# Queries and keys of a gated delta rule kept by features, with their norms and decays as broadcast rows instead of transposes in every chunk

## The reference

```
lower = where(strict, (k*beta) @ k^T * decay, 0);  tinv = (lower + I)^-1
u = tinv @ (v*beta);   w = tinv @ (k*beta*exp(g))
qk = where(causal, q @ k^T * decay, 0)
v_new = u - w @ state
o = (q*exp(g)) @ state + qk @ v_new
state = state * exp(g_last) + (k*exp(g_last - g))^T @ v_new
```

## Time and profile before

| | us |
|---|---|
| median of 3 runs | 1813.22 (1810.52 to 1816.22) |
| the profiled execution, device time | 1814.77 |
| its span from first to last instruction | 1812.9 |
| PE busy | 1732.7 (96%) |
| DVE, ACT, POOL busy | 910.4, 662.6, 483.4 |

### The profile page before, as it was taken

How to read it: one execution, slowest core, us unless ns; L and a number is a source line. 1 busy time by engine, 2 the same in 40 slices (tenths; PEclk the granted TensorE clock), 3 DMA queues, 4 the chain that set the end, 5 groups by cost and what they waited for, 6 DMA issues and landing times.

```text
span 1812.9 us, 31814 instructions
## 1 busy us (share of the span) xinstructions
PE 1732.7 (96%) x12561; PEld 1661.0 (92%) x12561; DVE 910.4 (50%) x1007; ACT 662.6 (37%) x1081; POOL 483.4 (27%) x470
## 2 busy tenths in 40 slices
PE   6999999986999999999969989999999999999997
PEld 6999999976999999999969989999999999999996
DVE  5454444563455544554452355455455455455457
ACT  6444474344455445444432342122222212212213
POOL 3222222223444354334402112122122122222220
PEclk9999999998999999999989999999999999999998
DMA  6233333224233423344295102111111111111112
GB/s 184 74 87 92 91 87 95 78 96 149 68 90 97 124 85 96 72 120 118 69 283 169 32 17 61 44 43 61 35 47 57 35 55 49 35 58 46 35 46 93
DMA packets 209164, 148.38 MB, mean 82 GB/s; under 512 B 43165, under 2 KB 197556, under 8 KB 207973
## 3 DMA queue, kind: packets, MB, share of 16 engines
q1 hardware_dynamic: 168052, 116.24, 22.3%
q10 hardware_dynamic: 40848, 31.49, 5.7%
q0 software_dynamic: 224, 0.12, 0.0%
HBM read 110.25 MB, written 37.58 MB: 82 GB/s over the span
## 4 chain that ended last, share of the span: by engine, by line
PE 80%; DVE 6%; issue 4%; DVEq 3%; DMA 2%; ACT 2%; POOL 1%; POOLq 1%; SPq 0%; ACTq 0%
PE gb L717 60%; PE db L1044 8%; PE db L853 3%; DVEq L1459 3%; PE db L850 2%; PE db L770 1%; DVE h L1841 1%; DMA yo<-ot_d 1%; PE db L923 1%; PE db L922 1%; DVE cacc L1496 1%; DVE hx L1769 1%; POOL w_lo L614 1%; PE db L997 1%; DVE fino L1875 0%
## 5 line engine op out<-in xcount | busy, mean ns | idle before, releaser
L717 PE MATMUL gb<-u_hi,w_hi 128*128 128x342 f32 (+2 forms) x2520 | 827.1, 328 | 17.1 <-ACT ht L1368 6.6
L717 PE MATMUL gb<-u_lo,w_hi 128*128 128x342 f32 (+2 forms) x2520 | 811.8, 322 | 0.0
L717 PE MATMUL gb<-u_hi,w_lo 128*128 128x342 f32 (+2 forms) x2520 | 808.5, 321 | 0.0
L614 POOL TENSOR_TENSOR w_lo<-w_raw,w_hi 128x1024 fp32r<-128x1024 f32 x128 | 327.1, 2564 | 1043.6 <-ACT w_hi L1086 1043.6
L717 PEld LDWEIGHTS gb<-u_hi,w_hi 128*128 128x128 f32 x2520 | 479.2, 190 | 21.5 <-issue 18.7
L717 PEld LDWEIGHTS gb<-u_lo,w_hi 128*128 128x128 f32 x2520 | 479.7, 190 | 0.4
L717 PEld LDWEIGHTS gb<-u_hi,w_lo 128*128 128x128 f32 x2520 | 479.0, 190 | 0.0
L1841 DVE TENSOR_TENSOR h<-h,db 128x512 f32<-128x512 f32 x176 | 117.5, 685 | 56.9 <-PE db L1044 56.5
L1044 PE MATMUL db<-w_hi,a_hi 128*128 128x512 f32 x352 | 139.6, 397 | 4.3 <-DVE a_lo L1865 2.9
L1086 ACT ACTIVATE w_hi<-w_raw 128x1024 fp32r<-128x1024 f32 x128 | 133.5, 1052 | 14.7 <-ACT tm L1176 13.0
L1044 PE MATMUL db<-w_hi,a_lo 128*128 128x512 f32 x352 | 138.2, 393 | 0.0
(11 more groups left out here) (236 smaller groups left out, 1855.3 us busy)
## 6 DMA issues: line engine op xcount, KB each, us to landing
w_raw<-in_w_in SPq DMA_DIRECT2D x53, 512.0 KB, 4.3
w_raw<-in_w_up SPq DMA_DIRECT2D x44, 512.0 KB, 3.8
qkv_d<-tm ACTq DMA_DIRECT2D x24, 576.0 KB, 3.4
tk<-qkv_d SPq DMA_DIRECT2D x9, 1536.0 KB, 7.2
w_raw<-in_w_down SPq DMA_DIRECT2D x22, 512.0 KB, 3.3
ot_d<-ots ACTq DMA_DIRECT2D x9, 512.0 KB, 3.2
yb_d<-ybs ACTq DMA_DIRECT2D x8, 513.0 KB, 3.9
yl<-yb_d SPq DMA_DIRECT2D x8, 513.0 KB, 5.5
```

The lines of the kernel that those rows point to most:

```text
L614: pool.tensor_tensor(w_lo[:, n % SLOTS, :], w_raw[:, n % SLOTS, :], w_hi[:, n % SLOTS, :].bitcast(F32), ALU.subtract).then_inc(s_wlo, 1)
L717: mm = pe.matmul(gb[:, bank, 0:w], wt, u, start=(k == 0 and m == 0), stop=(k == KT - 1 and m == 2))
```

## The change

Queries and keys are stored a second time by features: ACT stores `sl` to `qkT_d` before it is transposed, and only keys and values go by tokens to `kv_d`. The norm and beta of a key (`FKB`) and g (`GCUM`) are turned to rows once, by two PE transposes in the pooling stage (`rowsb`, stored to `rows_d`). For each chunk SP loads `kT` and `qT` from `qkT_d` and the two rows broadcast to all 128 partitions (`brow`, `grow`). DVE multiplies them: `kbt` = `kT` x `brow`, `ex` = `grow` - mask, `kgt` = `kbt` x exp(`grow`), `qdt` = `qT` x exp(`grow`). The key's own norm in `ex` comes as a logarithm added to g (`GLN`); the query's norm is applied to the output (`FQ`, `FQ2`). The six transpose steps and their copies are gone.

KK of the next chunk is now the first step of an iteration, and the 27 pieces lie differently behind the steps. `bds` goes back, and the loads for the chunk after follow, after the load of `tk`. In the pooling stage KK of chunk 0 stands before the fourth projection, so the blocks of the first inverse are solved during the pooling products. The last iteration is written out apart from the loop; on DVE the first too.

```diff
-STEPS = ["P1", "TKN", "V", "TKB", "GROW", "KK", "TQ", "TKG", "O", "SU", "QK", "TQD", "OT"]
+STEPS = ["KK", "P1", "V", "O", "SU", "QK", "OT"]
...
-FILLS = {"P1": 2, "TKN": 0, "V": 1, "TKB": 0, "GROW": 1, "KK": 2, "TQ": 2, "TKG": 2, "O": 2, "SU": 2, "QK": 1,
-         "TQD": 2, "OT": 3, "X0": 1, "Y0": 2, "X1": 1, "Y1": 1, "X2": 1, "Y2": 1}
+FILLS = {"KK": 2, "P1": 2, "V": 2, "O": 3, "SU": 2, "QK": 2, "OT": 3, "X0": 2, "Y0": 2, "X1": 2, "Y1": 2, "X2": 1,
+         "Y2": 2}
...
+FIRST_PLAN = [("pool", j) for j in range(5)] + ["QK"] + [("pool", j) for j in range(5, KT)]
...
+            sp.wait_ge(s_plo, 4)
+            load_tk(0)
+            sp.wait_ge(s_ps["QK"], 2)
+            load_kT(1)
+            load_qT(1)
+            blocks_back(0)
...
+            def chunk_loads(n, last):
+                blocks_out(n)
+                sp.wait_ge(s_vb, n)
+                sp.wait_ge(s_kd, n)
+                load_tk(n)
+                blocks_back(n)
+                if not last:
+                    sp.wait_ge(s_ps["QK"], 2 * n + 2)
+                    load_kT(n + 1)
+                    sp.wait_ge(s_kb, n + 1)
+                    sp.wait_ge(s_qd, n + 1)
+                    load_row(brow, 1, n + 1, s_br)
+                    load_row(grow, 0, n + 1, s_gr)
+                    load_qT(n + 1)
...
+            def key_rows(c):
+                dve.wait_ge(s_kT, 16 * c + 16)
+                dve.wait_ge(s_br, 16 * c + 16)
+                dve.tensor_tensor(kbt[:, :, :], kT[:, :, :], brow[:, :, :], ALU.mult).then_inc(s_kb, 1)
...
+                    if name == "P1" and isinstance(i, int) and i == 0:
+                        first_inverse()
+                    if not last and name == "Y0":
+                        key_rows(i + 2)
+                    elif not last and name == "X1":
+                        decays(i + 2)
```

More of the change, by code:

```diff
@@ L681, in _, with chunk @@
             state_parts(0)
[L682 to L686, removed]
+            w_low(W_ZG + 1)
+            pool.wait_ge(s_sst, 32)
+            w_low(W_ZG + 2)
+            def chunk(i, last):
                 substitute(i + 1)
+                if not last:
+                    pool.wait_ge(s_ev["QK"], 2 * i + 4)
+                    mask(i + 2)
                 pool.wait_ge(s_ps["SU"], 2 * i + 2)
@@ L915, in step @@
                     pe.wait_ge(s_ev["SU"], 2 * c + 2)
-                    each([done["TKG"]], product(kgt, st))
+                    pe.wait_ge(s_kg, c + 1)
+                    each([], product(kgt, st))
                 elif name == "V":
@@ L923, in both @@
                         return pe.matmul(o, qkm[:, m, :], vv[:, m, :], start=False, stop=True)
-                    each([done["V"], done["QK"], done["TQD"]], both)
+                    pe.wait_ge(s_qd, c + 1)
+                    each([done["V"], done["QK"]], both)
                 elif name == "SU":
@@ L975, in _ @@
                         piece(p, i)
+            with pe.Fori(0, HEADS - 1) as i:
+                chunk(i)
+            chunk(HEADS - 1)
             for name, prev in (("P1", LAST_Y), ("V", "P1"), ("O", "V"), ("OT", "O")):
@@ L1267, in copy_halves, with act_step @@
                     act.activation(heads(dst, h), dbank(name, h), ACT.Copy).then_inc(s_ev[name], 1)
-            def act_step(name, c):
-                if name == "TQ":
-                    copy_halves(name, qnt, c)
-                elif name == "TKN":
-                    copy_halves(name, knt, c)
-                elif name == "TQD":
-                    copy_halves(name, qdt, c)
-                elif name == "TKG":
-                    copy_halves(name, kgt, c)
-                elif name == "GROW":
-                    for h in range(2):
-                        act.wait_ge(s_ev[name], 2 * c + h + 1)
-                        act.activation(heads(ex, h), heads(ex, h), ACT.Exp).then_inc(s_dec, 1)
+            def act_step(name, c, last=False):
+                if name == "Y1" and not last:
+                    decays(c + 1)
                 elif name == "Y0":
@@ L1340, in _ @@
                 act.wait_ge(s_za, 16 * i + 16)
+            with act.Fori(0, HEADS - 1) as i:
+                chunk(i, False)
+            chunk(HEADS - 1, True)
             for name in REC:
@@ new lines, in _, with first_inverse @@
+            dve_step("QK", 0)
+            drain()
+            dve.tensor_tensor(ex[:, :, :], per_head(factor(GLN, 1)), over_heads(cst[:, C_NEG:C_NEG + P]),
+                              ALU.add).then_inc(s_nm, 1)
+            key_rows(1)
+            drain()
+            decays(1)
+            dve.drain().then_inc(s_ev[LAST_Y], 2)
+            def first_inverse():
+                dve.wait_ge(s_bd, 16)
+                dve.wait_ge(s_zero, 5)
+                for p in range(P // SQ):
+                    t = dve.transpose(rr[square(p), :, square(p)], bds[square(p), :, :])
+                t.then_inc(s_rd, 1)
```

440 lines of the change are left out of this document (244 added, 196 removed).

## The result

The changed kernel takes 1821.45 us (median of 7 runs, 1815.34 to 1823.92) against 1813.22: ratio 1.004, 95% interval 1.0023 to 1.0056. It is slower, by about 8 us (0.4%). The profiled execution is its fastest run, 1815.34 us with a span of 1813.5.

A forecast was written before the change was run, and what follows sets the result against it. PE alone was taken to bound the loop at 58.85 us an iteration. A 17.0 us gain at the start plus 7 x (58.85 - 55.2) = 25.6 gave 42.6, so 1772.2 profiled, 1771 median; range 1752 to 1794.

The forecast's parts named there:

- PE's own work: Chunk loop: 48 transposes removed save PE 5.7 us an iteration, so its period falls from 58.85 to 53.15 us.
- The chain from `gs` to POOL: Loop: weights issue to T + 7.4, blocks land T + 14.4 behind them, POOL starts T + 17.1.
- The substitution: POOL's solve in the loop: 12.9 us, plus 1.0 us for steps held by DVE products of two SBUF tiles.
- the strict reading: POOL's substitution: each DVE product with two SBUF inputs counts its full 1.25 us or so, giving a period of 56.6.
- Solution out and back: ... 5.1 us: Loop, from the substitution's end to X0: solution stored, reloaded and transposed in 5.1 us, so X0 can start at T + 35.1.
- The period is then 35.1 + 19.05: Loop: X0 at T + 35.1 plus 19.05 us of PE work behind it, 54.15 us; with POOL's held steps 55.2.
- the rival of the longer chain: Loop: weights and blocks crowd, period 57 to 60, time 1783 to 1804; chance 0.20 for 1782 to 1808.
- I leave its end at 418.7: Pooling stage: ACT's eight scalings start 1 us later but end as before; last store lands 422.6, P1 of chunk 0 at 425.0.
- The bound for this, 5 us: Pooling stage: QK and the loads of `kT` and `qT` may stretch the scalings by 5 us, cutting the gain to 12.
- The gain of 17.0: Start to end of iteration 0: ends at 479.5 in place of 496.47, 17.0 us gained, bounds 12 and 21.
- The broadcast rows: Loop: rival that row loads come late and PE stops before X1 and Y1 copies; 1837 us at 20 us landing; chance 0.06.
- The change moves nothing: Loop: rival that the way of the blocks eats just the transposes' time, needing a period near 61 us; chance 0.02.

The follow-up runs named there:

- the first experiment: On the changed kernel, SP sends the inverse's blocks out and back ahead of the three weight loads in the chunk loop: 1789.32 us, ratio 0.9872.
- that edit's base: Changed kernel with blocks ahead of weights, pooling-stage loads moved, and one gate-projection piece moved from behind OT to between QK and OT: 1770.67 us, ratio 0.9761.
- loads moved: On the changed kernel, chunk 0's QK right behind KK, so kT and qT load before the pooling stores; tk loads behind the last scaling: 1812.75 us, ratio 1.0008.
- the fastest version: Blocks first, pooling-stage loads moved, one piece moved ahead of OT; then chunk 0's KK and QK put behind the fourth pooling projection: 1763.54 us, ratio 0.9719.

## Why the prediction was wrong

1. **PE's own work: right.** 48 transposes for 5.7 us and a period of 53.15 without waits; 53.12 was measured once nothing else held the loop. By the mean duration of 275 ns it would have been 45.7.

2. **The chain from `gs` to POOL: right.** Forecast and measured, from KK at T: weights issued T + 7.4 and T + 8.0; blocks landed T + 14.4 and about T + 14.1, where their loads start; POOL's start T + 17.1 and T + 17.4. The first experiment shows what this queue order costs together with points 4 and 5, 4.3 us an iteration; without these two, with the outputs stored late, the order leaves 55.3 us, as forecast.

3. **The substitution: nearly right.** 12.9 + 1.0 = 13.9 forecast, 14.3 measured (631.59 to 645.87), with three held steps of 0.75, 1.02 and 1.17. A product costs up to 0.9 us, not the 1.25 of the strict reading of the Trainium skill (GPSIMD Engine Reference, Specifications); that fewer were allowed for is 0.4 us. The other direction, POOL's product holding one of DVE's, wasn't priced; by the traces it is behind the wait at OT in the first experiment, and behind the 3.1 and 3.4 us of `kbt` and `ex` of chunk 0 at the start.

4. **"Solution out and back: ... 5.1 us": the first failing step.** It was taken from the iteration before the change, where the way was clear. The change moved the solution later, onto ACT's 512 KB store of the outputs, and the two small stores then took 3.5 us in place of 1.7 and 1.9. From 645.90 to the end of `rrs` at 652.66 it was 6.8 us. X0 started at T + 38.6, PE was there at T + 34.25 (forecast 34.1). The prediction priced no meeting of DMAs from two engines on this leg. The Trainium skill (DMA: Bandwidth & Descriptors, Issuing engines are not separate DMA queues) says that DMAs of all issuing engines run on the same engines and interleave; the landing times here, 3.5 us beside the large store and 1.7 with it late, agree with that.

5. **"The period is then 35.1 + 19.05": the second failing step.** The 19.05 us behind X0 were matmuls at full clock. After a stop of 4.3 us part of them ran at 1.2 GHz, and X0 to KK took 21.2 us; where no stop of that length came before (X0 at 595.53) it took 18.7. With points 3 and 4 that is 59.74 for this iteration and 58.5 in the mean, against 55.2 forecast: 7 x 3.3 = 23 us. Summed over the seven, X0 starts 15.6 us too late, and what follows it takes 7.9 us too long. It ended in the rival of the longer chain (57 to 60), but for a cause that the rival didn't name; weights and blocks didn't crowd.

6. **"I leave its end at 418.7": the largest failing step.** The last store of the scalings was to land at 422.6 and landed at 439.0, 16.4 us later. By the rows: 5.6 us because the first started later, 8.7 because they stretched, 2.1 for the last one's landing (6.0 in place of 3.9). In all twelve changed versions P1 of chunk 0 starts 2.7 us behind this last landing (forecast 2.4), so the stores decide. The prediction let the scalings start 1 us later and end as before. They start late by PE's wait for `kbt` and the slow clock behind it, with KK ahead of the fourth projection, and, once that is gone, by DVE's products for chunk 0 ahead of the last pooled sums. With KK and QK behind the fourth projection the first store comes at 402.4, 1.5 us earlier than in the changed kernel (3.0 earlier than in that edit's base, where QK stood ahead too); the other 4.1 us are DVE's by the trace, and no run moved them. The stretch is the loads of `tk`, `kT` and `qT`: undone, 20.3 us remain of 29.1. The bound for this, 5 us, was worked from QK and the loads of `kT` and `qT`, and `tk` was overlooked. P1 of chunk 0 came at 441.8 in place of 425.0, iteration 0 ended at 500.7 in place of 479.5: 21 us, of which 4.4 lie behind P1. There the forecast had X0 wait for the third weight slot and the blocks, until 460.4; X0 started at 482.01 without a wait, and PE waited 4.3 us for `rr` in its place, which the prediction hadn't. The gain of 17.0 became a loss of 4.2.

The sum: 23 + 21 - 1.5 (the tail behind the last P1 was that much shorter) = 43 us, and the profiled run was to be 1772.2 and was 1815.3. That the median lies 6.1 us above the profiled run, where it lay 1.6 below, is the other 7.7 of the miss.

7. **The rivals and the signs.** The broadcast rows aren't late: `brow` and `grow` land 6.2 and 7.4 us after issue, like weights, and PE never waits at X1 to X2. "The change moves nothing" needed a period near 61; the time came out near that with 58.5, because the start lost what it was to win. Two signs of the forecast's own chain came: PE's repeated wait is the one before X0, ended by `rrs`, and the blocks land right behind the third weights. Of the signs of error, one came: the pooling stage ended behind 425, though by loads beside its stores and a late start, not by `bds`; with `bds` at 419 to 421 (loads moved) P1 still came at 435 to 438. The wait at OT on DVE's scaling isn't among the loop's repeated waits in the changed kernel; it comes when the blocks go first.

Left open: of the 6.8 us by which P1 of chunk 0 is still behind the forecast in the fastest version, 6.5 are the stores (402.4 to a last landing at 429.1). Why they land in 4.9 us in the median, and not in 4.3, with few loads beside them wasn't tried; nor was moving DVE's products for chunk 0 in the fastest version, or POOL's product away from DVE's small one.

## What to carry to other kernels

When an edit takes work from the bounding engine and hangs a chain through DRAM on the same loop, list every DMA of every engine by time and ask which ones the moved chain will now meet; here a small store issued 0.4 us behind a large one landed only when the large one had (3.5 us in place of 1.7). Price a new wait on PE twice, once for the wait and once for the matmuls behind it. When an edit makes one of POOL and DVE start its work earlier or later, look at what the other then does in the same microsecond. Where the start of a kernel is a pipeline of stores, put no load beside it and nothing that waits for another engine ahead of the matmuls that feed it.

## What the hardware showed unexpectedly

- **A large store doubles the landing time of small ones beside it.** Two stores of 32 KB land in 1.7 and 1.9 us alone and in 3.5 when 512 KB were issued 0.4 us before (the large one landed 3.8 us after its issue, just ahead of them); issued 0.8 and 0.5 us ahead of the large one they land in 1.7 and 1.9. Being ahead by less isn't enough: in the iteration with the stores at 764.05 and 764.40 and the large one at 764.46 the first lands in 1.7 us and the second in 3.8.
- **Stores beside loads.** The first `yb_d` store, 513 KB, took 9.1 us beside the 1 MB load of `tk`, and 4.5 without it.
- **The clock behind a wait.** The 15 matmuls behind X0 took 2.61 to 2.65 us after waits of 1.5 to 2.0 us, 3.5 to 4.6 after waits of 3.8 to 4.9, and either one after waits of 2.3 to 3.3. The granted clock had fallen to 0.50 by the time X0 started behind the wait of 4.31 us.
- **POOL beside a DVE product, and DVE beside POOL's.** A step of 0.21 to 0.29 us on POOL takes 1.0 to 1.2, three in a row when DVE has three such products in a row. A product of 8 columns on DVE takes 1.87 us in place of 0.17 when POOL's product of 1.90 us started 0.05 us before it, and 0.17 when it starts first.
- **A broadcast load is an ordinary load.** One 4 KB row read into each of 128 partitions, 512 KB in all, landed in 6.2 and 7.4 us in the iteration above, and in 4.3 to 8.3 over the run; the three weight loads of that iteration took 6.6 to 8.5.
